# Triangular solve in a two-layer decoder: products of levels 1 to 4 on four 32x32 tiles of TensorE's array

## What is computed

```python
a = jnp.einsum('bhncd,bhnsd->bhncs', k_beta, k) * decay
a = jnp.where(strict, a, 0.0) + jnp.eye(CHUNK, dtype=f32)
rhs = jnp.concatenate([v_beta, k_beta * jnp.exp(g)[..., None]], axis=-1)
sol = lax.linalg.triangular_solve(a, rhs, left_side=True, lower=True, unit_diagonal=True)
u, w = sol[..., :dv], sol[..., dv:]
...
def step(state, inp):
    qe_i, w_i, u_i, a_i, k_i, gl_i = inp
    v_new = u_i - jnp.einsum('bhck,bhkv->bhcv', w_i, state)
    o = jnp.einsum('bhck,bhkv->bhcv', qe_i, state) + jnp.einsum('bhcs,bhsv->bhcv', a_i, v_new)
    state = state * jnp.exp(gl_i)[..., None, None] + jnp.einsum('bhck,bhcv->bhkv', k_i, v_new)
    return state, o
```

## Time and profile before

| | us |
|---|---|
| median of 3 runs | 1526.05 |
| lowest and highest | 1525.6, 1527.71 |
| the profiled execution | 1529.22 |
| its span, first to last instruction | 1527.4 |
| PE busy | 1514.1 |
| DVE busy | 1174.1 |
| ACT busy | 928.9 |
| POOL busy | 121.9 |

### The profile page before, as it was taken

How to read it: one execution, slowest core, us unless ns; L and a number is a source line. 1 busy time by engine, 2 the same in 40 slices (tenths; PEclk the granted TensorE clock), 3 DMA queues, 4 the chain that set the end, 5 groups by cost and what they waited for, 6 DMA issues and landing times.

```text
span 1527.4 us, 21261 instructions
## 1 busy us (share of the span) xinstructions
PE 1514.1 (99%) x8444; PEld 1269.6 (83%) x8444; DVE 1174.1 (77%) x1081; ACT 928.9 (61%) x861; POOL 121.9 (8%) x85
## 2 busy tenths in 40 slices
PE   9999999999999999999999999999999999999998
PEld 7899989999985668888888888888888888888886
DVE  5987475444444569898898898998988988988985
ACT  3455445344323447777776777687777777777673
POOL 0481020000011000000000000000000000000000
PEclk9999999999999999999999999999999999999999
DMA  5413497455454349999999999999999999999990
GB/s 188 143 58 111 146 328 253 171 190 196 166 191 141 111 179 350 380 370 375 388 380 376 383 379 374 389 381 362 392 385 359 390 388 344 394 394 358 398 382 29
DMA packets 186683, 445.64 MB, mean 292 GB/s; under 512 B 5382, under 2 KB 5663, under 8 KB 186618
## 3 DMA queue, kind: packets, MB, share of 16 engines
q1 hardware_dynamic: 182336, 430.36, 76.3%
q0 software_dynamic: 3936, 14.20, 3.2%
q10 hardware_dynamic: 346, 0.15, 0.1%
HBM read 437.86 MB, written 7.89 MB: 292 GB/s over the span
## 4 chain that ended last, share of the span: by engine, by line
PE 94%; DVE 3%; ACT 1%; DMA 0%; issue 0%; POOL 0%; DVEq 0%; ACTq 0%; POOLq 0%
PE bank L1363 13%; PE bank L1365 13%; PE bank L1364 13%; PE bank L1350 7%; PE bank L1348 7%; PE bank L1349 7%; PE bank L651 4%; PE bank L1027 3%; PE bank L1026 3%; PE bank L1025 3%; PE bank L1149 2%; PE bank L1066 2%; PE bank L1013 1%; PE bank L1014 1%; PE bank L1015 1%; PE bank L727 1%
## 5 line engine op out<-in xcount | busy, mean ns | idle before, releaser
L2367 DVE TENSOR_TENSOR ring_r<-ring,buf_r 128x2048 fp32r<-128x2048 f32 x336 | 751.4, 2285 | 31.4 <-ACT buf_r L1732 31.4
L1732 ACT ACTIVATE buf_r<-ring 128x2048 fp32r<-128x2048 f32 x336 | 629.4, 1915 | 52.0 <-PE bank L1350 42.8
L1363 PE MATMUL bank<-ring_r,buf_r 128*128 128x512 f32 x896 | 354.5, 396 | 0.2 <-DVE buf_r L2486 0.2
L1365 PE MATMUL bank<-buf_r,buf_r 128*128 128x512 f32 x896 | 349.6, 390 | 0.0
L1364 PE MATMUL bank<-buf_r,buf_r 128*128 128x512 f32 x896 | 349.0, 389 | 0.0
L1365 PEld LDWEIGHTS bank<-buf_r,buf_r 128*128 128x128 f32 x896 | 168.2, 188 | 35.9
L1364 PEld LDWEIGHTS bank<-buf_r,buf_r 128*128 128x128 f32 x896 | 168.6, 188 | 33.7
L1363 PEld LDWEIGHTS bank<-ring_r,buf_r 128*128 128x128 f32 x896 | 168.2, 188 | 33.4 <-DVE buf_r L2486 0.3
L1348 PE MATMUL bank<-ring_r,buf_r 128*128 128x512 f32 x440 | 172.8, 393 | 0.0
L1350 PE MATMUL bank<-buf_r,buf_r 128*128 128x512 f32 x440 | 171.5, 390 | 0.0
L1349 PE MATMUL bank<-buf_r,buf_r 128*128 128x512 f32 x440 | 171.2, 389 | 0.0
(11 more groups left out here) (344 smaller groups left out, 1880.0 us busy)
## 6 DMA issues: line engine op xcount, KB each, us to landing
ring<-in_moe_w_gate SPq DMA_DIRECT2D x56, 2048.0 KB, 9.2
ring<-in_moe_w_up SPq DMA_DIRECT2D x56, 2048.0 KB, 9.1
ring<-in_moe_w_down SPq DMA_DIRECT2D x56, 2048.0 KB, 9.1
ring<-in_a_w_in SPq DMA_DIRECT2D x8, 2048.0 KB, 8.3
ring<-in_dense_w_gate SPq DMA_DIRECT2D x7, 2048.0 KB, 8.7
ring<-in_dense_w_up SPq DMA_DIRECT2D x7, 2048.0 KB, 7.9
ring<-in_dense_w_down SPq DMA_DIRECT2D x7, 2048.0 KB, 7.9
ring<-in_a_w_out SPq DMA_DIRECT2D x2, 2048.0 KB, 11.0
```

Of the source, the lines that this page charges most:

```text
L1363: pe.matmul(o, xh, low[:, c], start=k == 0, stop=False)
L1365: ins = pe.matmul(o, xh, high[:, c], start=False, stop=k == KT - 1)
L1732: act.activation(HB[m % NHB], half_words(m, U_MOE), ACT.Copy).then_inc(m_wh, 1)
L2367: dve.tensor_tensor(half_low(m, U_MOE), half_words(m, U_MOE), HB[m % NHB], ALU.subtract).then_inc(m_wl, 1)
```

## The change

The products y and z of levels 1 to 4 take the four 32x32 blocks on the diagonal in place of the two 64x64 ones, so four tiles of 32 rows and 32 columns each are used. Up to level 4 the blocks that are joined lie within these. The number of products in such a batch goes from 32 to 64, and their size from 64x64x64 to 32x32x32. DVE's subtraction at these levels takes the same four blocks: four operations of 32 partitions x 4 units x 32 columns per group in place of two of 64 x 4 x 64. Levels 5 and 6 keep their tiles, and no instruction changes its place in the order.

```diff
@@ -814,6 +814,10 @@
             HP = P // 2
             low, top = slice(0, HP), slice(HP, P)
 
+            def diagonal(lv):
+
+                return [slice(a, a + HP // 2) for a in range(0, P, HP // 2)] if lv < NLEV - 2 else [low, top]
+
             def turn(lv):
                 for g in range(4):
                     pe.wait_ge(u_ready, 4 * lv + g + 1)
@@ -836,7 +840,7 @@
                         if lv == NLEV - 1:
                             m = pe.matmul(quad(g, i)[top, low], R[1][low, u, top], R[4][low, u, low], start=True, stop=True)
                             continue
-                        for z in (low, top):
+                        for z in diagonal(lv):
                             m = pe.matmul(quad(g, i)[z, z], X[0][z, u, z], R[4][z, u, z], start=True, stop=True)
                     m.then_inc(y_mm, 1)
                 project(6 + lv, range(1))
@@ -844,7 +848,7 @@
                     pe.wait_ge(y_ready, 4 * (lv - 1) + g + 1)
                     for i in range(4):
                         u = 4 * g + i
-                        for z in (low, top) if lv < NLEV - 1 else (top,):
+                        for z in diagonal(lv) if lv < NLEV - 1 else (top,):
                             c = z if lv < NLEV - 1 else low
                             m = pe.matmul(quad(g, i)[c, z], X[3][z, u, c], R[3][z, u, z], start=True, stop=True)
                     m.then_inc(z_mm, 1)
@@ -2000,7 +2004,7 @@
                     elif lv == NLEV - 2:
                         parts = [(slice(0, 32), slice(32, 64)), (slice(64, 96), slice(96, P))]
                     else:
-                        parts = [(slice(0, 64), slice(0, 64)), (slice(64, P), slice(64, P))]
+                        parts = [(slice(a, a + 32), slice(a, a + 32)) for a in range(0, P, 32)]
                     for z, c in parts:
                         r = R[3][z, quads(g), c]
                         last = dve.tensor_tensor(r, r, as_quad(g)[z, :, c], ALU.subtract)
```

## The result

The changed kernel takes 1533.05 us (median of 20 runs, 1527.33 to 1536.91) against 1527.66 for the kernel before beside it (20 runs, 1525.60 to 1529.77): ratio 1.0032, 95% interval 1.0025 to 1.0038. It is slower by more than the 0.2% that can be told from no change, and lies above the whole forecast range (1520.8 to 1528.5). The forecast was set against 1526.05, the median of three runs, and the 20 runs of the kernel before have theirs 1.6 higher; taken as a difference, -2.9 us was forecast and +5.4 us measured.

A forecast was written before the change was run, and what follows sets the result against it. PE was taken to bound the changed levels (idle 1.03 of 50.6 us), DVE close behind. Terms 1.29 - 1.62 - 1.07 - 1.47 = -2.9 us, set against the median 1526.05, gave 1523.1 us, range 1520.8 to 1528.5.

The forecast's parts named there:

- every wait kept: Levels 1 to 4: starts of PE, DVE and ACT were moved in program order with every wait kept, giving -2.9 us.
- If four tiles work side by side as two do: Product batches y and z, levels 1 to 4: a batch takes 1.20 us, 0.81 less than 2.01.
- Rival B: Products y and z: tiles take turns, a batch takes 3.9 us; +13.5, 1539.6 us; chance 0.14.
- Level 1, +1.29: End of level 1: DVE's longer subtraction delays the last transposes and the start of level 2 by 1.29 us.
- Levels 2, 3 and 4, -1.62, -1.07, -1.47: Shorter products y and z save 1.62, 1.07 and 1.47 us, less waits for ACT's copies and, in level 3, the low part.
- Rival A: Products y and z: a batch gets hardly shorter, staying at 2.01 us; only +1.29 is left, 1527.3 us; chance 0.33.
- Does it reach the end?: Behind the solve: no wait for a load is on PE, so its work moves up as a whole by 2.9 us.
- theory F: Put up after the measurement, not forecast: PE's instructions arrive in blocks of 256, about one block ahead; 2 MB loads delay fetches.

The follow-up runs named there:

- undisturbed kernel: Changed kernel with level 1 left as before, four 32x32 products at the head, weight loads of units 5 and 6 held back: 1526.63 us, ratio 0.9998 against before.
- experiment 5: Kernel before with 384 products of 32x32, then 160 of 64x64, on constant data ahead of the program: 1563.86 us, a single execution.
- experiment 2: Changed kernel with weight loads of units 5 and 6 issued only after the y batches of levels 2 and 4: 1529.10 us, ratio 1.0009 against before.
- moved by 128: Changed kernel with 32 tiny products at the program's head, shifting later instructions by 128 places: 1532.33 us, ratio 1.0029 against before.

## Why the prediction was wrong

The step that failed is "every wait kept": the sum had no term for bringing PE its instructions, and none for half clock, which is seen inside or within 1.9 us behind 7 of the 12 stops of over 1 us. Taken with the profiled executions, the forecast for levels 1 to 4 was -2.9 and the trace shows 57.54 - 50.60 = +6.9. Of the gap of 9.8, the two stops are 1.91 + 5.03 = 6.9. Behind the second, PE worked 5.46 us at a clock of 0.51, which I estimate at 5.46 x 0.49 = 2.7 of lost work. That leaves 0.2 for all the terms of the sum together, which are -2.7 in the trace. The rest of the span moved by -1.5 ahead of the solve and +0.5 behind it, and 6.9 - 1.5 + 0.5 = 5.9 is the difference of the spans. The -1.5 is chance: a stretch at half clock that begins at about 23 us lasts 6.8 us in the profile of before and 3.4 in that of after, on the same instructions.

- **"If four tiles work side by side as two do, a batch takes 32 x 0.033 + 0.14 = 1.20 us": right.** It took 1.27: where nothing stops it, product z of level 2 starts at 96.50 and the projection behind it at 97.77, in level 3 107.34 and 108.61. Rival B, the tiles taking turns at 3.9 us, did not happen: the four row tiles write one bank, their records last 0.195 us each, and 128 of them are through in 1.3 us.
- **Level 1, +1.29: right** (+1.19, and +1.3 with DVE's part alone).
- **Levels 2, 3 and 4, -1.62, -1.07, -1.47: right to 0.4** once stops and clock are out: 0.66 - 1.91 = -1.25, -1.02, and 6.11 - 5.03 - 2.68 = -1.60. That the four terms add to -2.7, so near -2.9, is in part that level 2 gave less and level 4 more. In the undisturbed kernel the three are -1.41, -1.00 and -0.69, with 0.67 of waiting in the last.
- **"Every wait kept", ahead of the sum: here it failed.** I moved PE's starts by the waits that the trace of before shows and gave PE its instructions for nothing, since no row of before shows it without them. The change lets a batch eat 256 instructions in 1.3 us, where the fastest block of before's solve lasted 6.6, and PE's supply, which took 3.3 to 4.0 us a block in these traces where the DMA engines were idle, had no term.
- **Rival A came near, and had the wrong form.** It asked whether the engine can take products off its queue at one per 17 ns, for which there was no row, and priced a slower pace as a batch that stays at 2.01 us, so at worst +1.3. What the runs show is a supply in blocks and not a slower pace: at full clock a batch of 128 records takes 1.3 us where nothing stops it, and the stops listed in levels 1 to 4 last 0.16 to 5.03 us. That is why its price did not reach the result.
- **The clock, which had no term.** The earlier trace rows have it at full speed nearly throughout, and I priced a fall at nothing. In the mean over the runs it fell from 0.9979 to 0.9957, by the estimate above the larger part of the loss, 3.4 of 4.5 us.
- **"Does it reach the end?": yes.** From level 5 on the profiled executions differ by 0.5 us in 1400.

What was to be seen beforehand: the page of before lists queue 8 with 47 packets of 16 KB, the change adds 1024 instructions, and a batch would go from 128 of them in 2.0 us to 256 in 1.3. That is a rate of 200 instructions in a us where no batch of before's solve has over 64.

**What stays open.** The moment of a fetch against PE's entering a block is not fixed. For the border at record 122 of level 2's product y, the packet came at 87.19 with levels 2 to 4 alone, 0.9 us before PE entered the block ahead of that border, and at 88.85 with the loads held, 1.2 us behind it, though the DMA engines were idle there (share 0.02 from 86 to 92 us). For the blocks that stopped PE, it came between 0.1 us ahead of and 1.7 us behind PE's entering the block ahead where the DMA engines were idle, and 3.2 to 3.9 where a load filled them in z of levels 2 and 4; in the changed kernel it was 1.6 and 6.0. So a load delays it as theory F has it, but by how much it does not tell. Hence the size of a stop, and whether there is one, was not forecast well: the stop of level 2 did not shrink when the loads were held, and did not appear with levels 2 to 4 alone. Why idle time is followed by half clock in some executions and not in others was not tried.

## What to carry to other kernels

Small tiles multiply instructions: the 256 products more of this change are 1024 records more. So price a batch not only by the array but by the instructions that it takes from the queue, and against what the traces show of their supply. Here a batch on four tiles took 256 instructions (64 products of fp32) in 1.3 us, where the row of products of experiment 5 got as many every 3.7 to 4.0 us, and in 6.5 us once with the DMA engines busy at 0.97. Change the batches that leave the supply its time: level 3 has a border in each of its batches, but 4.2 us apart and with no load in flight (DMA share 0.06), and alone it took 0.12% off where the whole of the change cost 0.32%. In these traces the sign was a wait with releaser "issue" in the middle of a batch that waits for nothing, and the test was to put a few small products at the program's head: four of them moved both stops of the changed kernel from y to z of levels 2 and 4, which speaks for the supply.

## What the runs showed of the hardware

- Queue 8 moved packets of 16 KB (0.84 MB in 51 in the changed kernel), and their number rose with PE's instructions, by 1, 4, 5 and 9 for 256, 1024, 1152 and 2176 more (level 3 alone, changed, moved by 128, experiment 5): 256 to a packet, by estimate. A product in fp32 shows as four instructions, two records of PE and two of PEld.
- In the row of 384 products of 32x32 of experiment 5, PE stopped 5 times, from one stop to the next 256 instructions. The period was 3.7 to 4.0 us with the DMA share at 0.03 (20 to 30 us), and 6.5 us behind the first stop, with the share at 0.97 (10 to 20 us).
- All 18 stops of these profiles (13 in levels 1 to 4, 5 in experiment 5) end 2.25 to 2.67 us after a packet of queue 8 begins.
- The longest stop, 5.03 us in the changed kernel, had its block fetched at 118.14, from the middle of a 2 MB load; with that load moved (experiment 2) it was gone.
- Four 32x32 tiles worked at the same time, with one PSUM bank for all: 128 records of 0.195 us each in 1.3 us at full clock (the changed kernel, z of level 2), and 128 in 1.93 us at a clock of 0.50 (experiment 5).
- Of the 12 stops of over 1 us in levels 1 to 4, 7 had a fall to half clock inside them or within 1.9 us of their end, and 5 had none. In the changed kernel PE had stood for 3.6 us when the granted clock fell to 0.51 at 119.10, and it stayed there for 6.9 us; with the loads held PE had stood for 0.9 us when it fell at 90.4. A stop of 1.91 us, in the changed kernel, had none behind it.
